# First retrieval units of two heads, and half of the queries between the first weighted sums

## The reference, cut to what matters

```python
q = (xc @ wq).reshape(PEER_CHUNK, PEER_HEADS, 2, half)
sc = jnp.einsum('chpd,hpnd->chpn', q, sub_keys, preferred_element_type=jnp.float32)
s1, i1 = lax.top_k(sc[:, :, 0], PEER_TOPK)
s2, i2 = lax.top_k(sc[:, :, 1], PEER_TOPK)
...
top_s, pos = lax.top_k(cand, PEER_TOPK)
eidx = jnp.take_along_axis(cidx, pos, axis=-1)
g = jax.nn.softmax(top_s, axis=-1)
u_sel = jnp.take(u, eidx, axis=0)
a = jax.nn.gelu(jnp.einsum('chkd,cd->chk', u_sel, xc, preferred_element_type=jnp.float32), approximate=False)
w = (g * a).astype(x.dtype)
v_sel = jnp.take(v, eidx, axis=0)
return jnp.einsum('chk,chkd->cd', w, v_sel)
```

## Time and profile before

| | us |
|---|---|
| median of 3 runs | 3296.44 |
| profiled execution | 3295.42 |
| its span | 3293.6 |
| TensorE busy | 2508.8 (76%) |
| VectorE busy | 1621.7 (49%) |
| ScalarE busy | 833.0 (25%) |
| GpSimd busy | 834.5 (25%) |
| HBM traffic | 278 GB/s over the span |

### The profile page before, as it was taken

The page is one execution under the profiler, slowest core; times in us unless marked ns, Lnnn a source line. Parts: engine busy times, 40 slices in busy tenths (PEclk is TensorE's granted clock), DMA queues, the critical chain, the costliest instruction groups (busy, mean ns, idle before and its releaser), DMA issues.

```text
span 3293.6 us, 29030 instructions
## 1 busy us (share of the span) xinstructions
PE 2508.8 (76%) x9500; PEld 1324.6 (40%) x9500; DVE 1621.7 (49%) x3307; ACT 833.0 (25%) x2259; POOL 834.5 (25%) x717
## 2 busy tenths in 40 slices
PE   6788797877979868898877776868767676666564
PEld 3665343434545466533322222556543432222221
DVE  4545736769777553664758545364442421111112
ACT  1212334333433131223333333322110110101110
POOL 1002433344545200233444332020100111212221
PEclk9689998998989978999999999989988677878786
DMA  6027997897979702799999999101122488898884
GB/s 250 0 77 316 384 374 283 313 397 271 375 286 382 280 20 77 300 395 416 415 418 401 422 421 371 63 39 52 52 80 90 192 336 343 316 352 352 346 352 150
DMA packets 128898, 885.92 MB, mean 269 GB/s; under 512 B 23008, under 2 KB 23392, under 8 KB 31584
## 3 DMA queue, kind: packets, MB, share of 16 engines
q0 software_dynamic: 86976, 553.74, 42.8%
q1 hardware_dynamic: 41760, 330.22, 25.0%
HBM read 877.56 MB, written 37.75 MB: 278 GB/s over the span
## 4 chain that ended last, share of the span: by engine, by line
PE 47%; DMA 21%; DVE 19%; ACT 5%; issue 4%; POOL 2%; SPq 1%; DVEq 0%; POOLq 0%; ACTq 0%
PE ps L155 45%; DMA ring<-in_peer_uv,idx_u 11%; DMA ring<-in_w_gu 8%; DVE ring L1255 5%; DVE arena L76 4%; ACT arena L125 3%; PE ps L158 2%; DVE arena L97 1%; DVE ring L76 1%; ACT L125 1%; DMA arena<-in_w_gu 1%; DMA ring<-in_w_in 1%; DVE iu L113 1%; POOL small L134 1%; DVE arena L1255 1%
## 5 line engine op out<-in xcount | busy, mean ns | idle before, releaser
L155 PE MATMUL ps<-ring,arena 128*128 128x512 f32 (+3 forms) x3200 | 1251.8, 646 | 337.5 <-ACT arena L125 175.1
L155 PEld LDWEIGHTS ps<-ring,arena 128*128 128x128 f32 (+2 forms) x3200 | 468.0, 182 | 1026.3 <-issue 655.8
L1255 DVE CUSTOM_DVE_ANT_0 ring<-ring,h 128x1024 f32<-128x1024 f32 x428 | 536.5, 1254 | 398.5 <-DMA ring<-in_peer_uv,idx_u 371.9
L2296 POOL DMA_INDIRECT ring<-in_peer_uv,idx_u x428 | 469.3, 1096 | 791.6 <-PE ps L155 660.1
L155 PE MATMUL ps<-arena 128*128 128x128 f32 (+7 forms) x2184 | 511.2, 426 | 205.3 <-ACT arena L125 82.5
L125 ACT ACTIVATE arena<-arena 128x1 f32<-128x1 f32 (+4 forms) x1121 | 307.9, 275 | 833.0 <-DVE arena L1255 747.6
L155 PEld LDWEIGHTS ps<-arena 128*128 128x128 f32 (+3 forms) x2184 | 298.9, 206 | 383.9 <-issue 160.7
L155 PE MATMUL ps<-ring,hT 128*128 128x512 f32 (+1 forms) x704 | 323.6, 616 | 43.6 <-DMA ring<-in_w_in 21.3
L76 DVE TENSOR_TENSOR arena<-arena,ps 128x512 f32<-128x512 f32 (+1 forms) x134 | 77.2, 576 | 552.7 <-ACT arena L125 460.6
L125 ACT ACTIVATE arena<-ps 128x512 f32<-128x512 f32 (+5 forms) x164 | 89.5, 546 | 868.3 <-PE ps L155 801.6
L125 ACT ACTIVATE arena<-cst,arena 128x128 f32<-128x128 f32 x512 | 205.5, 401 | 185.1 <-PE ps L155 145.8
(11 more groups left out here) (116 smaller groups left out, 1615.6 us busy)
## 6 DMA issues: line engine op xcount, KB each, us to landing
ring<-in_w_gu SPq DMA_DIRECT2D x100, 1024.0 KB, 16.9
ring<-in_w_down SPq DMA_DIRECT2D x50, 1024.0 KB, 23.3
ring<-in_w_in SPq DMA_DIRECT2D x22, 2048.0 KB, 9.4
arena<-in_w_gu SPq DMA_DIRECT2D x28, 1024.0 KB, 17.3
ring<-in_w_mod SPq DMA_DIRECT2D x12, 2048.0 KB, 10.4
ring<-in_peer_wq SPq DMA_DIRECT2D x8, 2048.0 KB, 7.9
arena<-in_w_down SPq DMA_DIRECT2D x14, 1024.0 KB, 23.1
ring<-in_w_o SPq DMA_DIRECT2D x6, 2048.0 KB, 15.0
```

Source lines behind the costliest of these rows:

```text
L155: return self.e.matmul(o, lhsT, rhs, start=start, stop=stop, skip_group_check=True)
L1255: v.done(v.e.tensor_tensor_reduce(out=row, in0=row, in1=h[:, n // 128, :], scale=1.0, scalar=0.0, op0=ALU.mult, op1=ALU.add, accum_out=aa[ ...
L2296: g.e.indirect_dma_start(out=landing(n), out_offset=None, in_=d["peer_uv"], in_offset=bass.IndirectOffsetOnAxis(ap=idx_u[:, n:n + 1], axis ...
```

## The change

Units 0 and 1 have two heads each, the others stay at four (`UNITS` gives half, score blocks from and to, first slot; `UNIT_OF` the unit of a slot). Unit 0 is routed as soon as its one block of scores is there. Only query blocks 0 and 1 of both halves and the scores of units 0 and 1 stay up front; blocks 2 and 3 and the other six score blocks (`late`) stand behind weighted sums 0 to 23, a quarter of a query block or a score block at a time. The routing of units 1 to 4 stands beside the dot products by `ROUTE_AT`. The background begins at n = 25, and from n = 192 a step stands behind every second iteration (80 steps in layer 0 and 10 in layer 1, as before). Keys move to ring rows 14 and 15, the first gather lands in rows 12 and 13, and the ln2 rows are loaded when the keys have been used. The context, in_w_mod and what follows wait behind them.

```diff
-UNITS = [(0, 0), (0, 1), (1, 0), (1, 1)]
-ROUTE_PIECES, EXP_AT, WEIGHTS_AT = 24, 50, 54
+
+UNITS = [(0, 0, 1, 0), (0, 1, 2, 32), (0, 2, 4, 64), (1, 0, 2, 128), (1, 2, 4, 192)]
+UNIT_OF = [u for u, (c, j0, j1, n0) in enumerate(UNITS) for _ in range(32 * (j1 - j0))]
+
+ROUTE_AT = [[], [n for n in range(1, 23) if n % 3], [n for n in range(25, 56) if n % 3],
+            list(range(66, 108, 2)), list(range(130, 172, 2))]
+EXP_AT, WEIGHTS_AT = (-1, 20, 50, 114, 178), (1, 26, 58, 118, 182)
+LATE_QUERIES = 24
...
-        return 1 if n in range(4, 104, 10) else 0
-    return 1 if n in range(4, 130, 3) or n in range(138, 252, 3) else 0
+        return 1 if n in range(25, 125, 10) else 0
+    return 1 if n in range(25, 130, 3) or n in range(138, 192, 3) or n in range(192, 246, 2) else 0
...
-            i = n % GATHERS
+            i = (n + 4) % GATHERS
...
-                keys = R(12, 2)
+                keys = R(14, 2)
...
+                        if m == 3:
+                            pe.done(t, ("ps", "q", l, i, c))
+                            if c == 1:
+                                pe.tell(("used", "wq", l, i))
+                        yield
...
+                def late():
+
+                    for c in range(2):
+                        yield from queries(2, c, OTHERS)
+                        yield from queries(3, c, OTHERS)
+                        for j in (2, 3) if c == 0 else range(4):
+                            yield from scores(c, j, OTHERS)
+                        yield
...
-                for hf in range(2):
-                    for c in range(2):
-                        if hf == 0 and c == 0:
-                            turned_rows(0)
-                        queries(2 * hf, c)
-                        queries(2 * hf + 1, c)
-                        if hf == 0 and c == 0:
-                            turned_rows(1)
-                        scores(c, hf)
+                turned_rows(0)
+                run(queries(0, 0))
+                second_block = queries(1, 0)
+                next(second_block)
+                run(scores(0, 0))
+                run(second_block)
+                turned_rows(1)
+                run(scores(0, 1))
+                run(queries(0, 1))
+                run(queries(1, 1))
+                others = late()
                 for n in range(256):
                     if n % 128 == 0:
                         two = [fresh("acc", l, n // 128, x, among=SUMS[n // 128]) for x in range(2)]
                     weighted_sum(n, two)
+                    if n < LATE_QUERIES:
+                        next(others)
...
                 for _ in route(0):
                     pass
+                pieces = [route(u) for u in range(5)]
                 first = finish(0)
                 for n in range(256):
                     dots(n)
-                    if n == 1:
-                        weights(0)
-                    q, k = n // 64, n % 64
-                    if q < 3:
-                        if k == 1:
-                            pieces = route(q + 1)
-                        if k in range(2, 2 + 2 * ROUTE_PIECES, 2):
-                            next(pieces, None)
-                        if k == WEIGHTS_AT:
-                            weights(q + 1)
+                    for u, when in enumerate(ROUTE_AT):
+                        if n in when:
+                            next(pieces[u])
+                    if n in WEIGHTS_AT:
+                        weights(WEIGHTS_AT.index(n))
...
-                    i = n % GATHERS
-                    g.wait_ge(*at("idx", l, n // 64))
+                    i = (n + 4) % GATHERS
+                    g.wait_ge(*at("idx", l, UNIT_OF[n]))
                     if n >= GATHERS:
                         g.wait_ge(*at("used", "gather", l, n - GATHERS))
                     else:
-                        g.wait_ge(*at("used", "wq", l, i // 2) if i < 4 else at("used", "keys", l))
+                        g.wait_ge(*at("used", "wq", l, i // 2) if i < 4 else at("used", "w_o", l, 0))
...
-                block(12, 2, d["peer_keys"][l], ("loaded", "keys", l), after=[("used", "w_o", l, 0)])
-                row(14, 5 + 5 * l, ("loaded", "ln2", l, 0))
-                row(15, 6 + 5 * l, ("loaded", "ln2", l, 1))
+                block(14, 2, d["peer_keys"][l], ("loaded", "keys", l), after=[("used", "w_o", l, 0)])
                 block(16, 4, d["peer_wq"][l, 2], ("loaded", "wq", l, 2), after=[("used", "w_o", l, 1)])
                 block(0, 4, d["peer_wq"][l, 3], ("loaded", "wq", l, 3), after=[("used", "gn", l), ("used", "ln1", l)])
                 before = [("used", "wq", l, 3), ("used", "wq", l, 2)]
+                row(14, 5 + 5 * l, ("loaded", "ln2", l, 0), after=[("used", "keys", l)])
+                row(15, 6 + 5 * l, ("loaded", "ln2", l, 1))
```

More of the change, by code:

```diff
@@ L550, in turned_rows, with queries @@
                         turn4(b, lambda k: h[:, c, k * P:(k + 1) * P], k0, "hT", s, c, k0)
-                def queries(i, c):
-                    b = fresh("q", l, i, c)
+                def queries(i, c, among=range(8)):
+                    b = fresh("q", l, i, c, among=among)
                     pe.wait_ge(*at("loaded", "wq", l, i))
@@ L1953, in weigh @@
                     a.act(w, w, ACT.Gelu)
-                    a.wait_ge(*at("weights", l, n // 64))
+                    a.wait_ge(*at("weights", l, UNIT_OF[n]))
                     a.act(w, w, ACT.Copy, scale=gs[:, n:n + 1])
```

120 lines of the change are left out of this document (65 added, 55 removed).

## The result

The changed kernel takes 3311.19 us (median of 5 runs, 3303.33 to 3314.76) against 3296.44 before: ratio 1.004, 95% interval 1.0027 to 1.0054. Measured a second time it took 3306.58 us (10 runs) against 3296.09, ratio 1.0028 (1.0018 to 1.0038). The forecast of 3300 us is 7 to 11 us short; the range holds the result, and the sign is that of the forecast's +4, with a size between it and the upper end of its own range (3312).

The account below looks back on a forecast made before the run. The prediction took DMA engines to bound layer 1's loop and neither engine alone layer 0's, where it counted TensorE's idle time. Layer 0's +10 and layer 1's -6 made +4 on 3295.4: 3299 to 3300 us, range 3272 to 3328.

Parts of the forecast that it names:

- First gathers 22.6 us earlier: Start of each layer: routing begins 6.9 us earlier and takes 18.7 us instead of 34.4, so gathers leave 22.6 us earlier.
- the start wait of 11 us: Layer 0, ahead of the first weighted sum: TensorE idles 11 us against 3.43 before, costing +7.6 us.
- rival 4: Landing areas come free late, so first gathers leave no earlier and layer 1 loses its 22.6 us: 3323 us, chance 0.04.
- The clock's +3: Layer 0's start: after an 11 us wait, one to two weighted sums run slower, +3 us (between 0 and 6).
- TensorE bound in the first 24 iterations, +14 us of idle DMA engines: Layer 1, queries between weighted sums 0 to 23: DMA engines idle 15 us against 1 before, +14 us.
- Start of layer 1, -22.6: Layer 1's DMA book: gathers start 22.6 us earlier, counted as a gain of the full 22.6 us.
- The wait for in_w_mod, +6.6 in layer 0: Layer 0, first background step at n = 25: TensorE waits 13.5 us for the block against 6.9 before, +6.6 us.
- What the data-bound stretch gives back, -5: Layer 0, behind the in_w_mod wait: transfers run on, so later waits for data shrink, -5 us (0 to -16).
- rival 1: Head start partly kept: layer 0's early waits are repaid and the context chunk's new place helps; 3277 to 3282 us, chance 0.21.
- Context states' new place, -6: Layer 0: the heavy first context chunk starts at n = 159 instead of 138, away from other work, -6 us (0 to -10).
- The 27 steps two sums apart, 0: Layer 0 from n = 192: background steps behind every second weighted sum cost nothing, their chain being hidden by 3.6 us.
- rival 3: Layer 0's squeezed end is bound by the context states' chain, 27 steps costing 1 us or so more each: 3325 us, chance 0.20.

## Why the prediction was right in its size, and wrong in its steps

- **First gathers 22.6 us earlier.** Right: 23.1 and 23.2, counted from the first query. VectorE began the routing at 218.39, 7.7 us earlier by that count (forecast 6.9), and the routing took 18.9 us (18.7). The slices called empty, the third and the sixteenth, read 2 tenths in the earlier trace rows; the gap is read rightly from the earlier trace rows. Right, too, was the first weighted sum (251.29, forecast 254), the start wait of 11 us (11.52; the term was +7.6 and came to +8.1), so rival 4 is out. The clock's +3 came too: the first weighted sum has 3.37 us where the earlier trace rows have 1.98, and the 16 matmuls behind the wait for in_w_mod 9.15 us, against 7.03 without the wait (the row at 336.06 with in_w_mod first).
- **TensorE bound in the first 24 iterations, +14 us of idle DMA engines.** The mechanism is there, but smaller than the term: the share was 0.90 and 0.91 and not 0.7 to 0.8, and the size agrees only because a wait that the term did not contain fell into the same stretch: from 1355 to 1455 us the loads run at 346 GB/s and not at 404, which is 5.8 MB or 14.1 us. But only a part of it is the queries: with in_w_mod first the same 100 us have 387 GB/s, 4.1 MB more and thus 10 us, and the spread queries bring the last 2.3 MB, 5.6 us.
- **Start of layer 1, -22.6.** Too large. The gathers' lead is worth the bytes that they move, not the time by which they leave: in the first 67 us 208 GB/s against 102, 7.1 MB, 17 us. My book counted the DMA engines as busy from the first gather on; with six landing areas, and the first areas coming free only from the first weighted sum (1333.31) on, they are not: from 1334 to 1344 us their share is 0.77 and 0.73 in two windows of 5 us.
- **The wait for in_w_mod, +6.6 in layer 0.** This is the step that failed. It came out as 17.9 us, not 13.5 (a landing of 22.0 us, not 18.5), and it stands in layer 1 as well, with 11.5 us (14.5 in the second trace), where I had no term for it. The issue slipped behind the keys' last use in both layers, the ln2 rows stand in front of it in both, and I read the order of SyncE for layer 0 alone. Issued first and 27 us earlier, the blocks are worth 30 us in all, 11 of them by the order alone.
- **What the data-bound stretch gives back, -5.** TensorE's waits for gathered rows from 276 to 505 us fell by 15 us, from 33.3 (the earlier trace rows and 8.4 us behind them) to 18.3, but that is not the long wait's gift: without it they are 19.7. It gave back 1.4; the other 13.6 are TensorE's own work, now in their place. So in TensorE's book the early waits are filled as rival 1 had it. Its time of 3277 to 3282 us was not reached by that alone: with the two waits down to 5.2 and 3.7 us the kernel still took 3294.11, and only the earlier issue brought 3276.57.
- **Context states' new place, -6.** Not found. TensorE's waits from 505 to 705 us fell from 44.5 to 37.0 us, those from 705 to 905 rose from 32.5 to 37.4, and over all from 505 us on they fell by 3.4. The changed table of background steps by itself costs 6 us (1.0018, 1.0008 to 1.0029).
- **The 27 steps two sums apart, 0, and rival 3.** No sign of 25 us: from 505 to 1097 us TensorE is busy 493 us as against 497, and layer 0's length is known within 7 (889.4 to 896.1 in three traces). The tail term of +4 was not tested by itself.
- **Layer 0's busy time, taken as unchanged.** It was not: TensorE is busy for 751.3 of 889.0 us before, and for 746.5 of 894.0 and 741.7 of 889.5 in the two traces of the changed kernel, with 2760 matmul records and a granted clock of 0.94 in each. So 5 to 10 us came back that no term had, in spite of the two slower rows above. What made them was not tried and stays open.
- **Sums by layer.** Forecast +10 and -6, measured +5.0 and +2.4 in one trace, +0.4 and +7.2 in the other. By bytes layer 1 of the first trace is -17 for the head start (forecast -22.6), +14.1 for the next 100 us (+14, where queries and in_w_mod share it), +2.5 for the ln2 rows and +3.9 for the lower rate, which no term had: +3.5. In layer 0 the wait for in_w_mod came to 4.4 us more than forecast, the context states' -6 is not found, and the lower busy time makes up for them. The total, +7.5 in the layers by both traces, +10 to +15 by the medians, stands near the forecast because errors of unlike sign met: the queries were priced too high in layer 1 and the busy time in layer 0, while the head start was priced too well and in_w_mod too low or, in layer 1, at nothing. That is luck. The number was closer than its reasons.
- **The two rules.** The Trainium skill, "DMA: Bandwidth & Descriptors", section "Where 436 GB/s comes from", has 358 GB/s for a core's loads from HBM. The runs here, with one core at work, contradict it: 424 GB/s over 65 us in the kernel with in_w_mod first. (The 7 us that the prediction worked out from this figure should be 8: 16 x (3.59 - 2.93) is 10.6, against 19.) By the section "Queues, rings and completion order" of the same page of the Trainium skill, turns between queues packet by packet, the estimate was a landing of 20 us; 22.0 were measured. The traces agree with the rule within a quarter: the table of landings has 9.1 to 10.6, 16.1 to 19.1 and 22 us, where half of 411 GB/s gives 10.2, 15.3 and 20.4. I should have taken it.

## What to carry to other kernels

When a change moves the last use of a buffer, follow the load that waits for this buffer on its issuing queue, with all that stands behind it, in every layer and not only in the one looked at first: here that was worth 30 us, two to three times what the change cost by the medians. A head start for transfers is worth the bytes it moves before the steady state, and is lost if the engine that frees the landing areas is itself busy or stalled; fill the idle transfer time with other loads that don't need those areas (14 us here). When an engine's work is put into a loop bound by data, spread it at the pace that the data leave free; that was worth 5 us of layer 1 here, and is not told from noise in the whole kernel. And a change of several parts is best taken apart: the small units, together with in_w_mod first, are the part that was shown to pay, and the queries between the sums are not.

## What the runs showed of the hardware

- A block load next to a running gather queue moves at about half the rate (51.1% of the engines' time from 330 to 352 us in the changed kernel): 9.1 to 10.6, 16.1 to 19.1 and 22 us for 2, 3 and 4 MiB, of which 411 GB/s alone would need 5.1, 7.7 and 10.2.
- The loads of the one core at work, gathers and blocks together, reach 424 GB/s over 65 us and 410 over 100.
- With six gathers of 1 MiB done and no weighted sum yet to free an area, the DMA engines stand still (share 1.01 from 248 to 256 us, 0.00 from 264 to 276, with all queries up front), and 4 MiB of plain loads issued there in each layer saved 14 us in all.
